# A third ready-made u tile in each attention head of a hybrid decoder layer

## The chip, the cores and the metric

The kernel runs on one core of one Trainium2 chip. The metric is the device time of one launch in microseconds (us), the median of several runs. TensorE (PE), VectorE (DVE), ScalarE (ACT), GpSimd (POOL) and SyncE (SP) run their own instruction streams and wait for each other on semaphores; SP, ACT and POOL issue DMAs.

## What is computed

One decoder layer on 512 tokens of width 2048: eight differential-attention heads and a short convolution side by side, an output projection, and then a PEER mixer that picks, per token and query head, 16 of 16384 single-neuron experts. The last step is this, cut from the reference:

```python
def one_block(args):
    hb, eb, gb = args
    ug = jnp.take(u, eb, axis=0)
    vg = jnp.take(v, eb, axis=0)
    act = jax.nn.gelu(jnp.einsum("tkd,td->tk", ug, hb), approximate=False) * gb.astype(hb.dtype)
    return jnp.einsum("tk,tkd->td", act, vg)
```

## The kernel before, in words

The program has five stages, one behind another: the projection to q, k and v; a loop over the eight heads, in which each head also computes one eighth of the convolution; the output projection; the *sweep*; and a dense stage with the v table.

**The sweep.** Instead of gathering u rows for three of the four token blocks, the kernel multiplies the whole u table with the hidden rows of 384 tokens: 128 tiles of 128 experts. A tile is loaded as rows (`u_tile`), but the product needs it turned (experts along the free side). TensorE turns a tile itself with 16 transposes of 128x128 (`turned`, L2054), in two halves of eight, between the two halves of the products of the tile before. `uT_hi` and `uT_lo`, the two parts that the product takes (three matmuls for one fp32 product, L1804 to L1806), are made by ACT and DVE from what was turned. The sweep is written as eight times 16 tiles; the eighth has neither new queries nor a choice of experts in it.

**Ready-made tiles.** Some tiles are turned long before the sweep, in the first three stages. SP loads the rows of a tile (`near_rows` or `far_rows`, one buffer each), DVE turns them with four STREAM_TRANSPOSE of 128x512 (`turn_rows`, L1295), and four DMAs of 256 KB store the result in `uT_all` in HBM (`store_turned`, L454), by SP or, in the heads, by POOL. `turned_before` says which tiles of the sweep these are: the odd ones below 2 * TURNED. TURNED is 56 before the change, so that the odd tiles 1 to 111 come ready-made, and in the eighth sweep of 16 TensorE turns every tile. For a ready-made tile `split_u` of ACT (L1112) and DVE (L1642) reads `u_tile` in SBUF; for the others it reads PSUM (L1117, L1647).

**A head.** Each head takes six conv pieces of 512 KB: SP loads piece p (`conv_piece`, L561) when piece p-2 has been split, ACT makes `wc_hi` (L910) and DVE `wc_lo` (`split_wc`, L1263). The order on DVE is written by hand: pieces 3 and 4 (counted from 0, so "the fifth piece" is number 4) at the head's start, then the softmax of four query blocks by `biased(qb)` (L1399 to L1404) and `combined(qb)` (L1411 to L1415), piece 5 and pieces 0 and 1 of the next head among them, then the norms of the head's output and of the next q and k, piece 2 of the next head, and the gating of the convolution. TensorE fills the waits of the attention with conv matmuls: conv(1, 1, 4, 10), for example, stands between the scores of blocks 0 and 1 and `turn_a(0)` (L1897), which waits for `combined(0)`.

Two tiles are made ready in a head. I call them by their place on DVE: before the change one is turned in two parts, behind `combined(0)` and behind `combined(1)`; the other behind the norm of the head's output, ahead of `norm_qk(j + 1, 1)`. Their rows come by `next_rows` (L468) behind the load that follows piece p = 2 and behind the one that follows p = 5; `next_rows` waits until the tile before it has been turned, since there is one row buffer. The turned rows have one buffer too: `turn_rows` waits for the store of the tile before. `keep_turned` on POOL stores them and stands in one stream with the inverse roots of the norms, the 16 DMAs that zero the gate grid and the stores of the mix. The last head makes no tile ready.

## Time and profile before

| | us |
|---|---|
| median of three runs | 2991.14 |
| lowest and highest | 2988.70, 2996.27 |
| the profiled execution: its time | 2991.42 |
| its span | 2989.6 |
| busy in the span: PE, DVE, POOL, ACT | 2897.0, 2357.7, 1495.1, 1049.9 |
| the heads' loop, from the q and k norm of head 1 to that of head 6 | 207.28 |

The span is the time from the first to the last instruction in the profile. A row of the timeline has start, duration, engine, line, operation, what is written and read, and in brackets how long the engine sat idle before it and what ended that. The chain of work is followed back from the last instruction to whatever released it, so it shows at each time what the end depended on.

### The profile page before, as it was taken

The page shows a single profiled execution, that of the slowest core. Times are in us where ns is not written, and L with a number is a line of the kernel's source. Part 1 is how long each engine was busy: PE and PEld are TensorE (multiplying, and loading weights), DVE is VectorE, ACT ScalarE, POOL GpSimd, SP SyncE. Part 2 cuts the span into 40 slices and gives each one's busy share as a digit, 9 for nine tenths or more (in the row PEclk, how much of TensorE's full clock was granted, in tenths as well). Part 3 has the DMA queues.
Part 4 walks back from the last instruction along what each step waited for, and adds up shares of the span by engine and source line. Part 5 has one row for each costly group of instructions (what it writes and reads, how often), then busy time and mean ns, then how long its engine had stood idle before and what let it go on. Part 6 is the DMA issues. An engine that isn't in the chain of part 4 may idle for free.

```text
span 2989.6 us, 40571 instructions
## 1 busy us (share of the span) xinstructions
PE 2897.0 (97%) x14993; PEld 2575.2 (86%) x14993; DVE 2357.7 (79%) x3038; ACT 1049.9 (35%) x1373; POOL 1495.1 (50%) x906
## 2 busy tenths in 40 slices
PE   8999999999999999999999999999999999899998
PEld 6887777778889999999999999999997877777787
DVE  6445677755678888888888898899768998898898
ACT  4111433341323333433333343334223433333333
POOL 1000232200015656565565656566868887778662
PEclk9999999999999999999999999999999999999999
DMA  8998777778758998989999899999999999999998
GB/s 301 331 351 273 229 237 241 223 300 311 243 180 298 315 340 291 339 302 327 319 305 340 290 333 316 317 349 353 339 353 409 413 414 414 414 415 416 416 410 355
DMA packets 333295, 980.65 MB, mean 328 GB/s; under 512 B 63764, under 2 KB 180512, under 8 KB 241760
## 3 DMA queue, kind: packets, MB, share of 16 engines
q1 hardware_dynamic: 188560, 508.60, 46.3%
q0 software_dynamic: 107008, 439.75, 41.2%
q10 hardware_dynamic: 37584, 30.43, 3.1%
q8 instruction: 86, 1.41, 0.2%
q14 instruction: 57, 0.47, 0.0%
HBM read 866.33 MB, written 112.33 MB: 327 GB/s over the span
## 4 chain that ended last, share of the span: by engine, by line
PE 66%; DVE 14%; DMA 11%; issue 4%; ACT 3%; SPq 1%; ACTq 0%; DVEq 0%; POOL 0%
PE ps L1804 21%; PE ps L1806 20%; PE ps L1805 20%; DMA v_raw<-in_peer_v 8%; PE ps L2054 3%; DVE x_rows L1662 2%; DMA wc_raw<-in_w_in 2%; DVE v_lo L1704 2%; DVE u_row L1653 2%; ACT v_hi L1173 1%; DVE uT_lo L1642 1%; DVE x_one L1754 1%; DVE near_turned L1295 1%; DVE uT_lo L1647 1%; PE ps L1904 1%
## 5 line engine op out<-in xcount | busy, mean ns | idle before, releaser
L1804 PE MATMUL ps<-hT_hi,uT_hi 128*128 128x384 f32 x2048 | 701.0, 342 | 21.2 <-DVE uT_lo L1642 19.0
L1806 PE MATMUL ps<-h2T_lo,uT_hi 128*128 128x384 f32 x2048 | 688.0, 336 | 0.0
L1805 PE MATMUL ps<-hT_hi,uT_lo 128*128 128x384 f32 x2048 | 687.0, 335 | 0.0
L815 POOL DMA_INDIRECT gate_grid<-gates,grid_cells x256 | 524.6, 2049 | 107.5 <-issue 78.8
L1804 PE MATMUL ps<-v_hi,a_hi 128*128 128x512 f32 x1024 | 403.7, 394 | 35.5 <-DVE v_lo L1704 34.9
L1804 PEld LDWEIGHTS ps<-hT_hi,uT_hi 128*128 128x128 f32 x2048 | 386.2, 189 | 30.9 <-DVE uT_lo L1642 24.8
L1173 ACT ACTIVATE v_hi<-v_raw 128x2048 fp32r<-128x2048 f32 x128 | 245.7, 1919 | 453.0 <-PE ps L1806 338.6
L1805 PE MATMUL ps<-v_hi,a_lo 128*128 128x512 f32 x1024 | 401.1, 392 | 0.0
L1806 PE MATMUL ps<-v_lo,a_hi 128*128 128x512 f32 x1024 | 401.0, 392 | 0.0
L1805 PEld LDWEIGHTS ps<-hT_hi,uT_lo 128*128 128x128 f32 x2048 | 386.6, 189 | 1.9
L1806 PEld LDWEIGHTS ps<-h2T_lo,uT_hi 128*128 128x128 f32 x2048 | 386.0, 188 | 0.0
L834 POOL DMA_INDIRECT v_ring<-in_peer_v,experts x128 | 291.3, 2276 | 135.8 <-DVE x_one L1754 103.8
L1704 DVE TENSOR_TENSOR v_lo<-v_raw,v_hi 128x2048 fp32r<-128x2048 f32 x128 | 293.2, 2291 | 72.9 <-ACT v_hi L1173 69.7
L805 POOL DMA_INDIRECT v_row<-in_peer_v,experts x128 | 147.6, 1153 | 341.3 <-DVE x_rows L1662 309.4
L1754 DVE SCALAR_TENSOR_TENSOR x_one<-v_ring,acts,x_one 128x2048 f32<-128x2048 f32 x128 | 300.5, 2347 | 3.2 <-DVE acts L1739 2.2
L1662 DVE SCALAR_TENSOR_TENSOR x_rows<-v_row,acts,x_rows 128x2048 f32<-128x2048 f32 x128 | 300.1, 2344 | 0.8 <-ACT acts L1126 0.8
L1653 DVE CUSTOM_DVE_ANT_0 u_row<-u_row,h_rows 128x2048 f32<-128x2048 f32 x128 | 292.5, 2285 | 0.0
L823 POOL DMA_INDIRECT dots<-products_one,cells x128 | 259.8, 2030 | 39.0 <-issue 39.0
L1804 PEld LDWEIGHTS ps<-v_hi,a_hi 128*128 128x128 f32 x1024 | 194.0, 189 | 83.8 <-issue 34.2
L1647 DVE TENSOR_TENSOR uT_lo<-ps,uT_hi 128x1024 fp32r<-128x1024 f32 x144 | 176.2, 1224 | 111.7 <-ACT uT_hi L1117 103.5
L1117 ACT ACTIVATE uT_hi<-ps 128x1024 fp32r<-128x1024 f32 x144 | 148.0, 1028 | 319.4 <-PE ps L2054 282.8
L1804 PE MATMUL ps<-w_hi,hT_hi 128*128 128x512 f32 x624 | 244.0, 391 | 0.8 <-DVE wi_lo L1249 0.8
(207 smaller groups left out, 4958.7 us busy)
## 6 DMA issues: line engine op xcount, KB each, us to landing
v_raw<-in_peer_v SPq DMA_DIRECT2D x128, 1024.0 KB
u_tile<-in_peer_u SPq DMA_DIRECT2D x72, 1024.0 KB
u_tile<-uT_all SPq DMA_DIRECT2D x56, 1024.0 KB
near_rows<-in_peer_u SPq DMA_DIRECT2D x40, 1024.0 KB, 8.3
uT_all<-near_turned SPq DMA_DIRECT2D x100, 256.0 KB, 7.0
w_raw<-in_w_in SPq DMA_DIRECT2D x24, 1024.0 KB, 9.2
wc_raw<-in_w_in SPq DMA_DIRECT2D x48, 512.0 KB, 7.4
far_rows<-in_peer_u SPq DMA_DIRECT2D x16, 1024.0 KB, 9.4
```

Source lines behind the costliest of these rows:

```text
L815: pool.indirect_dma_start(out=gate_grid, out_offset=bass.IndirectOffsetOnAxis(ap=grid_cells[:, d, col:col + 1], axis=0), in_=gates[:, 2 + ...
L823: pool.indirect_dma_start(out=dots[:, s:s + 1], out_offset=None, in_=products_one, in_offset=bass.IndirectOffsetOnAxis(ap=cells[:, col:col ...
L834: pool.indirect_dma_start(out=v_ring[s % RING][:, :], out_offset=None, in_=v_table, in_offset=slot(1, h, s)).then_inc(v_in[s % RING], 16)
L1173: nc.scalar.activation(v_hi[b % 2][:, :], v_raw[b % RAW_RING][:, :], ACT.Copy).then_inc(v_hi_ready, 1)
L1647: v.tensor_tensor(uT_lo[half][:, :, :], ps_uT[half], uT_hi[half][:, :, :].bitcast(F32), ALU.subtract)\
L1653: v.tensor_tensor_reduce(out=u_row[c % 2][:, :], in0=u_row[c % 2][:, :], in1=h_rows[:, 0, :], scale=1.0, scalar=0.0, op0=ALU.mult, op1=ALU ...
L1662: v.scalar_tensor_tensor(out=x_rows[:, 0, :], in0=v_row[c % 2][:, :], scalar=acts0[:, b:b + 1], in1=x_rows[:, 0, :], op0=ALU.mult, op1=ALU ...
L1704: v.tensor_tensor(v_lo[b % 2][:, :], v_raw[b % RAW_RING][:, :], v_hi[b % 2][:, :].bitcast(F32), ALU.subtract).then_inc(v_lo_ready, 1)
L1754: v.scalar_tensor_tensor(out=x_one[:, :], in0=v_ring[s % RING][:, :], scalar=acts[:, s:s + 1], in1=x_one[:, :], op0=ALU.mult, op1=ALU.add) ...
L1804: mm(out, a_hi, b_hi, start=first, stop=False)
L1805: mm(out, a_lo, b_hi, start=False, stop=False)
L1806: return mm(out, a_hi, b_lo, start=False, stop=last)
```

## The change

Three tiles a head are made ready instead of two, so TURNED goes from 56 to 63, and the odd tiles 113 to 125 of the eighth sweep come ready-made as well. Tile 127 does not. The new place is in front of `split_wc(j, 4)`, in one part; the tile that was turned in two parts is now turned in one, behind `combined(1)`; the place behind the norm stays.

```diff
-KEPT_BY_POOL = 1 + 2 * (HEADS - 1)
+KEPT_BY_POOL = 1 + 3 * (HEADS - 1)
@@ SP @@
-                    if p in (2, 5):
-                        next_rows(NEAR, 2 * j + (NEAR_HEADS + p // 5))
+                    if p in (2, 4, 5):
+                        next_rows(NEAR, 3 * j + (NEAR_HEADS + (2, 4, 5).index(p)))
@@ POOL @@
                 if j < HEADS - 1:
-                    keep_turned(NEAR_HEADS + 1 + 2 * j)
+                    keep_turned(NEAR_HEADS + 1 + 3 * j)
+                    keep_turned(NEAR_HEADS + 2 + 3 * j)
...
-                    keep_turned(NEAR_HEADS + 2 + 2 * j)
+                    keep_turned(NEAR_HEADS + 3 + 3 * j)
@@ DVE @@
+                if not last:
+                    turn_rows(NEAR, 3 * j + (NEAR_HEADS + 1), "heads")
                 split_wc(j, 4)
...
                 combined(0)
-                if not last:
-                    turn_rows(NEAR, 2 * j + (NEAR_HEADS + 1), "heads", range(2))
                 biased(2)
                 combined(1)
                 if not last:
-                    turn_rows(NEAR, 2 * j + (NEAR_HEADS + 1), "heads", range(2, 4))
+                    turn_rows(NEAR, 3 * j + (NEAR_HEADS + 2), "heads")
                 biased(3)
...
                 if not last:
-                    turn_rows(NEAR, 2 * j + (NEAR_HEADS + 2), "heads")
+                    turn_rows(NEAR, 3 * j + (NEAR_HEADS + 3), "heads")
```

DVE at the start of a head, before (`wc_lo<-wc_raw_129` is piece 4, `alibi` and `conv_taps` are two small steps ahead of it; ISA rows are waits and parts of instructions):

```order
L1263 TENSOR_TENSOR wc_lo<-wc_raw_130,wc_hi 128x1024
L1387 TENSOR_SCALAR alibi<-alibi 128x512
L1388 ISA
L1388 COPY conv_taps<-vec 128x3
L129 ISA
L1262 REGISTER_ALU
L1263 TENSOR_TENSOR wc_lo<-wc_raw_129,wc_hi 128x1024
```

And with the change:

```order
L1264 TENSOR_TENSOR wc_lo<-wc_raw_130,wc_hi 128x1024
L1388 TENSOR_SCALAR alibi<-alibi 128x512
L1389 ISA
L1389 COPY conv_taps<-vec 128x3
L129 ISA
L1287 ISA
L1291 ISA
L1296 STREAM_TRANSPOSE near_turned<-near_rows 128x4x4x32 x4
L1263 REGISTER_ALU
L1264 TENSOR_TENSOR wc_lo<-wc_raw_129,wc_hi 128x1024
```

Two waits (for the rows, L1287, and for the store of the tile before, L1291) and four transposes now stand ahead of piece 4, and so ahead of the whole softmax of the head.

SP in the loop over the heads, behind the load that follows p = 4, with the change (before, neither the two ISA rows nor the load of `near_rows` stand here):

```order
L561 DMA wc_raw_129<-in_w_in 128x8x128
L473 ISA
L468 ISA
L468 DMA near_rows<-in_peer_u 128x2048
L572 REGISTER_ALU
L561 ISA
L561 DMA wc_raw_130<-in_w_in 128x8x128
```

The load of the second tile's rows is put between piece 0 and piece 1 of the next head. The load for the first tile stays where it was, behind piece 4.

## Rows read from the trace of the kernel before

**Rows 1.** The page: span of the profiled execution.
```profile
span 2989.6 us, 40571 instructions
```

**Rows 2.** Chain of work over the whole span (start us, us, what).
```profile
336.68 1.23 DVE qk_ss L1379
...
543.96 1.23 DVE qk_ss L1379
```

**Rows 3.** Chain of work through head 3, 420 to 462 us.
```profile
426.56 7.56 DMA wc_raw<-in_w_in
...
434.23 1.07 ACT wc_hi L910
...
438.96 0.36 DVE probs L1415
...
439.37 0.33 PE ps L1897
```

**Rows 4.** Timeline of DVE, 415 to 462 us.
```profile
432.05 0.63 DVE L1388 COPY conv_taps<-vec 128x3 f32 x1
435.32 1.23 DVE L1263 TENSOR_TENSOR wc_lo<-wc_raw,wc_hi 128x1024 fp32r<-128x1024 f32 x1 [2.64 <-ACT wc_hi L910]
...
439.23 1.30 DVE L1295 STREAM_TRANSPOSE near_turned<-near_rows 128x512 f32<-128x512 f32 x2
...
446.72 0.69 DVE L1399 CUSTOM_DVE_ANT_0 probs<-ps,alibi 128x512 f32<-128x512 f32 x1 [2.16 <-PE ps L1897]
```

**Rows 5.** Instructions on near_rows, window 427 to 428 us.
```profile
L468 SPq DMA_DIRECT2D near_rows<-in_peer_u x1: 1962/1962/1962, 427.3 to 427.3; - x1
...
DMA to landing us min/median/max: 10.2/10.2/10.2
```

**Rows 6.** The same in head 1, window 343 to 346 us.
```profile
DMA to landing us min/median/max: 9.9/9.9/9.9
```

**Rows 7.** The same in head 3, window 448 to 455 us.
```profile
L468 SPq DMA_DIRECT2D near_rows<-in_peer_u x1: 346/346/346, 451.8 to 451.8; - x1
...
DMA to landing us min/median/max: 5.7/5.7/5.7
```

**Rows 8.** Timeline of PE before turn_a(0) of head 3.
```profile
438.50 0.39 PE L1806 MATMUL ps<-hT_lo,wc_hi 128*128 128x512 f32 x1
439.37 0.33 PE L1897 MATMUL ps<-ident,probs 128*128 128x128 f32 x1 [0.48 <-DVE probs L1415]
```

**Rows 9.** Timeline of DVE in head 0: its piece 4.
```profile
309.11 1.23 DVE L1263 TENSOR_TENSOR wc_lo<-wc_raw,wc_hi 128x1024 fp32r<-128x1024 f32 x1 [5.32 <-ACT wc_hi L910]
```

**Rows 10.** Timeline of PE in the dense stage, after a stall.
```profile
2478.72 0.79 PE L1804 MATMUL ps<-v_hi,a_hi 128*128 128x512 f32 x1 [5.32 <-DVE v_lo L1704]
2479.31 0.63 PE L1805 MATMUL ps<-v_hi,a_lo 128*128 128x512 f32 x1
2479.73 0.63 PE L1806 MATMUL ps<-v_lo,a_hi 128*128 128x512 f32 x1
```

**Rows 11.** Windows: that stretch, all engines; PEclk is the granted clock.
```profile
2476.13:2482.94 6.81, 4.22 (x10) 3.36 (x11) 6.65 (x4) 2.56 (x3) 5.90 (x4) 0.50 1.02 421
```

**Rows 12.** Chain of work, seventh sweep of 16: uT_lo, every fourth tile.
```profile
1951.11 1.24 DVE uT_lo L1642
...
2065.36 1.24 DVE uT_lo L1642
```

**Rows 13.** Timeline of PE, eighth sweep: the transposes of a tile's half.
```profile
2070.93 1.03 PE L2054 MATMUL ps<-ident,u_tile 128*128 128x128 f32 x8
...
2091.12 1.03 PE L2054 MATMUL ps<-ident,u_tile 128*128 128x128 f32 x8
```

**Rows 14.** Chain of work, 2030 to 2072 us: the same transposes.
```profile
2052.02 0.87 PE ps L2054 x8
```

**Rows 15.** Windows, seventh and eighth sweep: PE, PEld, DVE, ACT, POOL busy, PEclk, DMA.
```profile
1913.00:2065.00 152.00, 149.16 (x899) 146.43 (x898) 143.47 (x224) 60.77 (x98) 100.91 (x64) 1.00 0.98 346
2065.00:2235.00 170.00, 169.49 (x1068) 167.85 (x1067) 125.17 (x105) 54.25 (x90) 116.89 (x71) 1.00 0.97 350
```

## Prediction

> **What bounds the kernel now.** I read the page first, then the chain of work, then timelines of one head and of the last two sweeps. The profiled execution took 2991.42 us with a span of 2989.6 [rows 1]; the median of the three runs is 2991.14, 0.3 us below it, so I sum against 2991.4. TensorE is the busiest engine nearly everywhere, and the question is what the change does to the two places that it touches.
>
> *The heads.* Five heads, from the q/k norm of head 1 to that of head 6, take 207.3 us, or 41.5 us each [rows 2]. The chain through a head [rows 3] is to be read link by link: piece 4 is issued at 426.56 and takes 7.56 us; ACT splits it at 434.23, DVE makes its low part behind that (435.32, [rows 4]), does block 0 of the softmax until 439.32, and only then TensorE can turn block 0 at 439.37. TensorE was there earlier: its last conv matmul ahead of it began at 438.50, and it idled 0.48 us [rows 8]. So between 426 and 439 us DVE's order holds the head, with TensorE less than a us behind. DVE has one hole on this way, 2.64 us between `conv_taps` (ends 432.68) and piece 4 (starts 435.32), in which it waits for ACT [rows 4]. This hole is the room into which the change puts the new tile.
>
> *The sweep.* In the seventh sweep, where every second tile is ready-made, 12 tiles take 2065.36 - 1951.11 = 114.25 us, 9.52 a tile [rows 12]. In the eighth, where TensorE turns all, two tiles take 2091.12 - 2070.93 = 20.19 us, 10.10 a tile [rows 13], and TensorE is busy 169.49 of 170 us [rows 15].
>
> **The gain: seven tiles of the eighth sweep.** Seven tiles lose their 16 transposes. The lower price of a tile: a pair took 19.04 us with one ready-made and 20.19 with none, so 1.15 us. The upper: eight transposes hold the chain for 0.87 us [rows 14], 16 for 1.74. In the seventh sweep DVE was busy 143.47 of 152 us, because it also chose experts, and TensorE had to wait for it; in the eighth it is busy only 125.17 of 170 [rows 15], so it should keep up better. I take 1.4 a tile, 7 x 1.4 = 10 us, with 8 and 12 as ends. ACT and DVE split a ready-made tile with instructions of the same kind on SBUF, at no extra price, covered by DVE's 45 free us. The u loads of the sweep stay the same in number and size.
>
> **The cost: the new place in front of piece 4.** The transposes alone would be free. Two take 1.30 us, so four take 2.6 [rows 4], and the hole is 2.64. But they need the rows, and the rows have come too late for it. The load that feeds this place is the one behind p = 2, and it is in the kernel already: issued at 427.28 behind piece 4, it landed 10.2 us later [rows 5], at 437.5. Before the change nobody noticed, as the first transposes came at 439.23 [rows 4]. Now DVE waits at its new place until 437.5, turns until 440.1, and then starts on piece 4, for 435.32 before: 4.8 us later. All of block 0's softmax is queued behind it, and TensorE behind that, so I charge the whole 4.8. The load behind p = 2 has this landing in each of heads 1 to 6, from 9.9 us up [rows 6] and all within 0.4 us, since each has the same traffic around it: the store of the tile before, piece 4 ahead in SP's own queue, and the zeroing of the gate grid. None of that moves. Six heads make 6 x 4.8 = 28.8 us. Head 0 has a hole of 5.32 us ahead of piece 4, which ends at 309.11 for another reason [rows 9], and its load was issued at 293.7; I cost it at nothing. Head 7 turns nothing.
>
> **The second cost: TensorE's clock.** TensorE's wait ahead of block 0 grows from 0.48 to some 5.3 us. The trace has a stall of 5.32 us in the dense stage [rows 10]. Around it the granted clock is 0.50 for 6.8 us, the lower level of 1.2 GHz [rows 11], and the matmuls behind the stall start 0.42 us apart (2479.31 to 2479.73), where the conv matmuls of a head stand at some 0.23. Ten such matmuls were counted in that stretch [rows 11], so a stall costs 10 x 0.2 = 2.0 us more. TensorE is the bound behind `turn_a(0)`, so I charge it: 6 x 2.0 = 12 us, with 0 and 12 as ends. The Trainium skill ("TensorE: Matmul & The Clock Gate", Part 1) says that an idle TensorE is put back to 1.2 GHz; by that rule, the trace agrees.
>
> **The other edits.** *The two-part tile becomes one behind `combined(1)`.* DVE idled 2.16 us ahead of `biased(3)` [rows 4], which covers the extra 1.3 us of transposes there. But its rows are now loaded behind p = 4, some 2 us behind the new tile's transposes, so at about 442.5, and `combined(1)` is through at about 448 in the new times. The row nearest in a quiet stretch lands in 5.7 us [rows 7], at 448.2; one as slow as [rows 5] would land at 452.7, and with 2.6 us of transposes `biased(3)` would come about 4 us later than TensorE wants it. DVE also waits for the new tile's store, which POOL can issue only from 440.1 on. I take 0, because TensorE at the lower clock arrives 2 us later itself; the upper end is 3 us a head, 18 in all. *The third load* stands behind p = 5 as before. *POOL* issues four more DMAs a head; it waits in most of a head, and the inverse root queued behind them is due 10 us later. I cost them at nothing; if that cover went, the roots, the next q and k and piece 2 would be late. *Piece 0 of the next head* is issued 5 us later, as everything behind piece 4; it is not needed before the head's last third.
>
> **Sum.** 2991.4 - 10 + 28.8 + 12 = 3022.2 us.
>
> **Rivals.**
>
> *A. The stall without the clock.* The 5 us stalls fall so that the granted clock stays at full, as the clock is not lost in every idle moment. Then 2991.4 - 10 + 28.8 = 3010. Against it: the stall of the same length in [rows 10].
>
> *B. The rows come in time, and the change is faster.* Mechanism: the row load of p = 2 lands as fast as the one of p = 5, in 5.7 us [rows 7], so at 433.0. Then DVE turns from 433.0 to 435.6 and is 0.3 us late with piece 4. The point that decides is a landing by some 433 us: below it the transposes fit in the hole, above it every us is paid once a head. Time: 2991.4 - 10 + 6 x 0.3 = 2983. For it: longer heads leave DMA more air. Against it: the load still stands right behind piece 4, and in six of six heads it needed 10 us.
>
> *C. The second wait too.* The rows or the buffer of the middle tile are late as well: 3 us more a head, 3022 + 18 = 3040. For it: two more MB of traffic a head, in a stretch where the queues are full until 444 us.
>
> *D. POOL holds the eighth sweep.* POOL scatters all gates of that sweep in its first 11 tiles. If it cannot go faster than 10.1 us a tile, five of the seven tiles give nothing, and the gain is 3 instead of 10 us: 3029. Against it: busy 116.89 of 170 us [rows 15]. The Trainium skill ("GPSIMD Engine Reference", section 8) says that GpSimd shares its SBUF interfaces with VectorE and contends with DVE instructions that have two SBUF inputs, as DVE's dots and sums have; the rows can't say how much of POOL's busy time is such waiting.
>
> *E. The change does nothing.* The order says otherwise: TensorE's stream is shorter by the seven tiles' transposes. I give this no chance of its own.
>
> **How the numbers follow.** A measurement of this kernel tells some 0.3%, 9 us, from no change. The forecast as summed has 0.50, A 0.20, C 0.10, D 0.05: all are slower by more than 9 us, 0.85. B has 0.09, faster by 8 to 12 us, of which I count 0.01 as same. The remaining 0.06 is a mixture: the rows land 2 us sooner in the longer heads and the clock holds, 6 x 2.8 - 12 = +5, the same. So faster 0.08, same 0.07, slower 0.85. The range goes from 3002 (3.6 us a head, no clock, gain 10) to 3038 (nearly all of C).
>
> **What would show it.** Right: in heads 1 to 6 DVE idles about 5 us behind `conv_taps` with the near_rows DMA as what ended it; TensorE's turn of block 0 has 5 us of idle before it; a head takes 46 to 49 us; PEclk drops in the heads; the eighth sweep is about 10 us shorter. Wrong: a landing of the p = 2 rows below 7 us; a head at 42 us; or an eighth sweep that has not moved, which would point to POOL or DMA.

## The result and the profile after

| | before | with the change |
|---|---|---|
| median of the runs, us | 2989.92 (4 runs, 2988.42 to 2996.27) | 3056.05 (4 runs, 3049.62 to 3059.38) |
| ratio, with its 95% interval | | 1.0216 [1.0202, 1.0229] |
| span of the profiled execution, us | 2989.6 | 3053.4 |

The change costs 66 us, or 2.2%. The direction was forecast; the size was not, as 3056 lies 18 us above the upper end of the range. The two spans differ by 63.8 us, and the rows below say where they lie. Lines of the changed kernel are mostly one higher than before (the wait of `turn_a` is L1898 for L1897).

**The heads: +55.3 us.** The squares for the q/k norm are summed once a head, so the first and the last of these sums frame seven heads.

The kernel before, instructions on qk_ss (line, engine, operation and count, shortest/median/longest ns, first to last start):
```profile
L1379 DVE TENSOR_REDUCE qk_ss<-sq x8: 1220/1220/1222, 294.1 to 585.4; 128x16 f32<-128x1024 f32 x8
```
The changed kernel, the same view:
```profile
L1380 DVE TENSOR_REDUCE qk_ss<-sq x8: 1220/1221/1222, 294.2 to 640.8; 128x16 f32<-128x1024 f32 x8
```
Seven heads took 291.3 us and take 346.6. Head 0 has hardly a part in that: the six heads behind it went from 248.7 us (336.7 to 585.4) to 302.9 (337.9 to 640.8). That is 54.2 us, or 9.0 a head, for the 6.8 of the forecast.

The changed kernel, waits of PE, 338 to 641 us (who <- what ended it: us in total, times, longest):
```profile
PE ps L1898 <- DVE probs L1418: 33.5, 10, 6.7
PE ps L1905 <- ACT aT L967: 6.9, 6, 1.3
```
The kernel before, waits of PE, 337 to 586 us:
```profile
PE ps L1897 <- DVE probs L1415: 1.9, 5, 0.5
```
TensorE waited 1.9 us in these six heads and waits 40.4 now: 30.8 at the turn of block 0 (6.70, 4.98, 4.82, 4.34, 4.99 and 4.96 us in heads 1 to 6), 2.7 at later turns and 6.9 for `aT`, ACT's copy of the turned blocks. So 38.5 of the 54.2 us are idle time of TensorE. The rest, 15.7 or 2.6 a head, is time in which it works more slowly, as the windows over the six heads show (PE, PEld, DVE, ACT, POOL busy, then PEclk, DMA share, GB/s), first before, then with the change:
```profile
336.70:585.40 248.70, 246.65 (x1214) 194.99 (x1213) 182.56 (x397) 98.02 (x193) 70.00 (x85) 1.00 0.76 241
337.90:640.80 302.90, 262.51 (x1214) 202.37 (x1213) 196.90 (x420) 96.46 (x193) 83.07 (x109) 0.94 0.75 239
```
The same 1214 matmuls are busy for 262.5 us instead of 246.7, at a granted clock of 0.94 in the mean instead of 1.00.

The changed kernel, waits of DVE, 338 to 641 us:
```profile
DVE near_turned L1296 <- DMA near_rows<-in_peer_u: 48.6, 12, 6.4
```
Before, DVE never waited for rows in these heads. Now it waits twelve times, so twice a head.

The changed kernel, timeline of DVE in head 3 (start, duration, what, in brackets the idle before it and what ended it; its first row is the same `conv_taps` step as the first row of [rows 4], which now comes 20.6 us later):
```profile
452.69 0.63 DVE L1389 COPY conv_taps<-vec 128x3 f32 x1
457.84 2.49 DVE L1296 STREAM_TRANSPOSE near_turned<-near_rows 128x512 f32<-128x512 f32 x4 [4.52 <-DMA near_rows<-in_peer_u]
460.25 1.18 DVE L1264 TENSOR_TENSOR wc_lo<-wc_raw,wc_hi 128x1024 fp32r<-128x1024 f32 x1
...
472.67 2.49 DVE L1296 STREAM_TRANSPOSE near_turned<-near_rows 128x512 f32<-128x512 f32 x4 [3.38 <-DMA near_rows<-in_peer_u]
475.08 0.65 DVE L1402 CUSTOM_DVE_ANT_0 probs<-ps,alibi 128x512 f32<-128x512 f32 x1
```
Between `conv_taps` and piece 4's `wc_lo` there now lie 4.52 us of waiting and 2.49 of turning, for the 2.64 us hole of [rows 4]. That is the forecast's mechanism. The second wait, 3.38 us in front of the middle tile, is the one that the forecast had taken as 0; `biased(3)` (475.08) stands behind it.

The changed kernel, instructions on near_rows, 447 to 449 us, the answer to [rows 5]:
```profile
L468 SPq DMA_DIRECT2D near_rows<-in_peer_u x1: 1885/1885/1885, 447.9 to 447.9; - x1
...
DMA to landing us min/median/max: 9.8/9.8/9.8
```
The same at 462 to 463 us, the middle tile's load:
```profile
L468 SPq DMA_DIRECT2D near_rows<-in_peer_u x1: 972/972/972, 462.3 to 462.3; - x1
...
DMA to landing us min/median/max: 10.2/10.2/10.2
```
The first load takes the 10 us that were read from the kernel before; the second, for which [rows 7] had suggested 5.7, takes 10.2.

The changed kernel, timeline of PE at the turn of block 0 in head 3:
```profile
464.37 0.47 PE L1898 MATMUL ps<-ident,probs 128*128 128x128 f32 x1 [4.82 <-DVE probs L1418]
```
And the window around it (PE, PEld, DVE, ACT, POOL busy, then PEclk, DMA share, GB/s):
```profile
459.00:465.80 6.80, 1.98 (x8) 0.81 (x6) 4.88 (x18) 2.25 (x9) 2.20 (x4) 0.72 1.05 354
```
The idle of 0.48 us in [rows 8] is 4.82, and the granted clock has a mean of 0.72 around it, so it is at 1.2 GHz for over half of those 6.8 us. The same window shows the DMA engines full (share 1.05).

**The eighth sweep: 5.3 us longer instead of 10 shorter.** ACT copies the product of each tile out of PSUM, so sixteen of these copies frame fifteen tiles. Instructions on products in the kernel before:
```profile
L1147 ACT ACTIVATE products<-ps x16: 490/492/492, 2086.3 to 2237.3; 128x384 f32<-128x384 f32 x16
```
The same in the changed kernel:
```profile
L1148 ACT ACTIVATE products<-ps x16: 490/492/493, 2144.0 to 2300.3; 128x384 f32<-128x384 f32 x16
```
They took 151.0 us and take 156.3.

The changed kernel, waits of DVE in this stretch:
```profile
DVE u_row L1654 <- DMA u_row<-in_peer_u,experts: 25.9, 9, 5.5
DVE x_rows L1663 <- DMA v_row<-in_peer_v,experts: 9.4, 4, 3.6
```
DVE never waited for a gathered row there before; now it waits 35.3 us for `u_row` and `v_row`. POOL issues these gathers, between its scatters of the gates.

The changed kernel, windows: the stretch in three parts (PE, PEld, DVE, ACT, POOL busy, PEclk, DMA share, GB/s):
```profile
2144.00:2210.00 66.00, 65.63 (x399) 64.73 (x399) 50.94 (x37) 23.27 (x37) 53.95 (x28) 1.00 0.97 341
2210.00:2262.00 52.00, 46.42 (x256) 44.70 (x255) 31.99 (x24) 14.44 (x25) 44.99 (x24) 0.93 0.93 308
2262.00:2300.30 38.30, 33.19 (x198) 31.91 (x196) 25.05 (x20) 8.68 (x16) 18.99 (x13) 1.00 0.94 348
```
In the first part TensorE has hardly a gap: its seven tiles took 65.5 us, for 70.7 before. In the second it stands still for 5.6 us of 52, and this is POOL's part: 24 issues are busy for 44.99 us, and with the 0.30 us that lies between two of them (7.2 in all) they fill the 52 us to the last. The next five tiles took 56.3 us, for 50.5. In the third part there are hardly any scatters left (the last is issued at 2269.94), but the gathered rows are still late: the last three tiles took 34.5 us, for 29.9. In the chain of work two gathers of `v_row` stand there with 9.15 and 13.68 us from issue to landing. So 4.7 of the 5.3 us come when the scatters are all but over; why the loop doesn't catch up there, no run shows.

The changed kernel, groups of POOL's instructions over the whole stretch (busy us, mean ns, idle before and what ended it):
```profile
L816 POOL DMA_INDIRECT gate_grid<-gates,grid_cells x32 | 73.6, 2299 | 9.7 <-issue 9.7
L801 POOL DMA_INDIRECT u_row<-in_peer_u,experts x15 | 26.3, 1755 | 14.7 <-DVE dots L1654 11.0 <-issue 3.7
L806 POOL DMA_INDIRECT v_row<-in_peer_v,experts x16 | 19.3, 1207 | 14.2 <-issue 8.9 <-DVE x_rows L1663 5.3
```
The same in the kernel before:
```profile
L815 POOL DMA_INDIRECT gate_grid<-gates,grid_cells x32 | 58.6, 1832 | 9.7 <-issue 9.7
L805 POOL DMA_INDIRECT v_row<-in_peer_v,experts x15 | 30.9, 2062 | 26.5 <-DVE x_rows L1662 18.0 <-issue 8.5
L800 POOL DMA_INDIRECT u_row<-in_peer_u,experts x15 | 14.8, 987 | 13.6 <-DVE dots L1653 9.9 <-issue 3.7
```
The same 32 scatters cost POOL 15 us more than before, while the gathers' issues together stay at 45.6 us (45.7 before).

The remaining 3 us of the 63.8 lie in the stretches between: 1.8 from the heads to the first product of the sweep, 0.5 in the first seven sweeps, 0.8 in the dense stage, each no more than one execution differs from another.

### The profile page after: what moved, and what is told of

It reads as the page before. It is cut to its first block, busy times and chain, and to the rows that moved or that the text cites. A ratio compares the mean times of both kernels' runs of the same rounds, so it can differ in the third digit from the quotient of the medians.

```text
span 3053.4 us, 40459 instructions
## 1 busy us (share of the span) xinstructions
PE 2911.7 (95%) x14881; PEld 2580.2 (85%) x14881; DVE 2375.2 (78%) x3066; ACT 1049.7 (34%) x1373; POOL 1522.3 (50%) x934
## 4 chain that ended last, share of the span: by engine, by line
PE 57%; DVE 16%; DMA 12%; issue 6%; POOL 5%; ACT 3%; SPq 0%; ACTq 0%; DVEq 0%; POOLq 0%
PE ps L1805 18%; PE ps L1807 18%; PE ps L1806 18%; DMA v_raw<-in_peer_v 6%; DVE x_rows L1663 3%; DMA near_rows<-in_peer_u 3%; PE ps L2055 2%; DVE u_row L1654 2%; POOL gate_grid L816 2%; DMA wc_raw<-in_w_in 2%; DVE v_lo L1705 2%; DVE near_turned L1296 1%; DVE uT_lo L1643 1%; ACT v_hi L1174 1%; POOL dots L824 1%
## 5 line engine op out<-in xcount | busy, mean ns | idle before, releaser
L816 POOL DMA_INDIRECT gate_grid<-gates,grid_cells x256 | 535.3, 2091 | 107.4 <-issue 78.8
L806 POOL DMA_INDIRECT v_row<-in_peer_v,experts x128 | 135.1, 1055 | 331.8 <-DVE x_rows L1663 306.0
L824 POOL DMA_INDIRECT dots<-products_one,cells x128 | 267.2, 2088 | 49.1 <-issue 38.7
L801 POOL DMA_INDIRECT u_row<-in_peer_u,experts x128 | 176.4, 1378 | 151.0 <-DVE dots L1654 75.5
L454 POOL DMA_DIRECT2D uT_all<-near_turned x88 | 48.5, 558 | 404.1 <-DVE near_turned L1296 403.0
```

Source lines behind the costliest of these rows:

```text
L801: pool.indirect_dma_start(out=u_row[b % 2][:, :], out_offset=None, in_=u_table, in_offset=slot(0, i, b)).then_inc(u_in[b % 2], 16)
L816: pool.indirect_dma_start(out=gate_grid, out_offset=bass.IndirectOffsetOnAxis(ap=grid_cells[:, d, col:col + 1], axis=0), in_=gates[:, 2 + ...
L824: pool.indirect_dma_start(out=dots[:, s:s + 1], out_offset=None, in_=products_one, in_offset=bass.IndirectOffsetOnAxis(ap=cells[:, col:col ...
```

## The experiments

Sixteen kernels, on chips where the kernel before took between 2991.65 and 2993.66 us in the median. Five take the sweep apart, the others the heads; *heads* below is the time from the first to the last sum of squares (291.3 us before, 346.6 with the change), and *eighth sweep* that of fifteen tiles (151.0 and 156.3). Both are read from the one profiled execution of each kernel; that of s1 was the slowest of its ten (3002.80 us) and that of s3 the slowest of its six, so their sweeps are long by some us.

| run | median, us | ratio [95%] | heads | eighth sweep |
|---|---|---|---|---|
| s1_sweep_only | 2995.50 | 1.0018 [1.0007, 1.0028] | | 159.8 |
| s2_low_from_psum | 2995.71 | 1.0018 [1.0007, 1.0030] | | 152.5 |
| s3_scatter13 | 3001.95 | 1.0038 [1.0025, 1.0050] | | 161.5 |
| s4_half_scatters | 2978.81 | 0.9956 [0.9939, 0.9972] | | 140.1 |
| c1_before_half_scatters | 2992.45 | 1.0000 [0.9988, 1.0013] | | 150.6 |
| h1_heads_only | 3051.13 | 1.0201 [1.0181, 1.0221] | 348.6 | 150.6 |
| h2_first_rows_small | 3054.58 | 1.0211 [1.0193, 1.0230] | 347.3 | |
| h3_second_rows_small | 3029.35 | 1.0120 [1.0103, 1.0137] | 331.3 | |
| h4_both_rows_small | 3030.55 | 1.0134 [1.0118, 1.0151] | 325.2 | |
| h5_zeroing_in_last_head | 3084.64 | 1.0312 [1.0295, 1.0330] | 350.8 | |
| h6_small_rows_ahead | 3022.34 | 1.0093 [1.0072, 1.0113] | 321.0 | |
| h7_full_rows_ahead | 3069.18 | 1.0256 [1.0233, 1.0280] | 364.2 | |
| h8_no_rows | 3018.49 | 1.0088 [1.0071, 1.0105] | 318.7 | |
| h9_small_rows_no_zeroing | 3022.85 | 1.0099 [1.0082, 1.0116] | 290.6 | |
| g1_other_places | 3022.65 | 1.0103 [1.0086, 1.0120] | 316.5 | 154.3 |
| g4_places_zeroing_last | 3058.79 | 1.0215 [1.0197, 1.0234] | 319.7 | 154.3 |

### The two parts of the change apart

**s1_sweep_only.** The kernel before, in which the sweep takes tiles 113 to 125 as ready-made. Their rows are those of tile 111, read again.
```diff
-    return tile % 2 == 1 and tile < 2 * TURNED
+    return tile % 2 == 1 and tile < 2 * (TURNED + 7)
...
-                    source = uT_all[tile // 2 * P:(tile // 2 + 1) * P, :] if turned_before(tile)\
+                    source = uT_all[min(tile // 2, TURNED - 1) * P:(min(tile // 2, TURNED - 1) + 1) * P, :] if turned_before(tile)\
```


> The kernel before, with only the sweep changed: the odd tiles 113 to 125 are also taken as ready-made (they re-read the stored rows of tile 111, so the products of these seven tiles are not the reference's); no third tile is made in the heads. Theory 1 (the missing 10 us were lost in the eighth sweep itself, where GpSimd cannot issue faster): the eighth sweep of 16 takes about 156 us instead of 151, GpSimd is busy nearly all of its first 11 tiles, and the time is 2 to 8 us above before. Rival (the sweep gains 8 to 12 us as I forecast, and the changed kernel lost it by something that the heads left behind): the eighth sweep takes about 141 us and the time is 8 to 12 us below before.

2995.50 us, 1.0018 [1.0007, 1.0028] of before. The gain isn't there even with heads that are as before: it is lost in the sweep itself, and nothing that the heads do takes it away.

**h1_heads_only.** The changed kernel, all 63 tiles made and stored, but the sweep uses the first 56.
```diff
-    return tile % 2 == 1 and tile < 2 * TURNED
+    return tile % 2 == 1 and tile < 2 * (TURNED - 7)
```


> The changed kernel with all its new work in the heads, but the sweep takes only the 56 tiles of before as ready-made, so that the seven new ones are made and not used. Theory 1 (the heads cost 55 us by themselves, and nothing in the sweep pays it back): heads 1 to 6 take 50 us each, the eighth sweep 151 us as before, and the time is 53 to 58 us above before. Rival (part of the loss needs the changed sweep, or the extra stores of the heads slow later stages): more than 3 us of the difference to before lies behind the heads.

3051.13 us: the heads alone cost some 60 us. So the two parts, 59 and 4 us over before, come to 63 of the change's 66. All heads runs below start from this kernel, if nothing else is said.

### The sweep: who holds it

**s2_low_from_psum.** As s1, but DVE makes `uT_lo` of the seven tiles from PSUM, as for the tiles that TensorE turns.
```diff
-                if turned_before(c):
+                if turned_before(c) and c < 2 * TURNED:
```


> As s1_sweep_only, but for the seven new ready-made tiles VectorE takes the low part from the PSUM bank (whatever stands there) instead of from u_tile in SBUF, so that its subtraction has one SBUF input and not two; the low part of these tiles is then not the reference's. Same instructions, same order. Theory A (GpSimd is held off by VectorE instructions with two SBUF inputs, of which the ready-made tiles add two a tile): GpSimd's gate_grid instructions get shorter than in s1_sweep_only, the eighth sweep falls from 156 to 148 us or less. Rival B (GpSimd is slow because the tiles come faster and its 3 scatters and 2 gathers a tile meet full DMA queues): the eighth sweep takes the same as in s1_sweep_only within 2 us.

2995.71 us, to s1's 2995.50. The two single profiles differ (152.5 and 159.8 us), the medians of the runs don't. So the source of the low part makes no difference in time that these runs can tell, and this edit does not bring the gain back.

**s3_scatter13.** As s1, with the last 32 scatters over 13 tiles instead of 11.
```diff
-                    tiles = TOPK - 1 if i < PEER_HEADS - 1 else 11
+                    tiles = TOPK - 1 if i < PEER_HEADS - 1 else 13
```


> As s1_sweep_only, but the last sweep's 32 scatters are spread over 13 tiles instead of 11, so 2.46 instead of 2.91 a tile. Theory 1 (GpSimd's issue time a tile sets the eighth sweep): it falls by some 0.45 x 2.3 us a tile in the first 11 tiles, so by about 10 us to 146 us, and the time is below before by some 5 us, unless the last scatters then come too late for the first weights of the dense stage. Rival (the bound in the eighth sweep is DMA bandwidth, not issue): no change to s1_sweep_only, as the bytes are the same.

3001.95 us, slower than s1 by 6. The expectation missed. With thinner scatters nine early tiles run at some 9.2 us instead of seven, but the last scatter is over only at 2227 us and the first dense gates are loaded behind it, at 2229. DVE waits 15.0 us for them in the last tile, which takes 24.7 us. The work of POOL was moved, not made less.

**s4_half_scatters.** As s1, with every second scatter of the eighth sweep left out.
```diff
+                        if i == PEER_HEADS - 1 and n % DENSE == 1:
+                            continue
```


> As s1_sweep_only, but the eighth sweep issues 16 of its 32 scatters of gates (those of one of the two dense token blocks are left out, so its gates are wrong); each moves 128 values of 4 bytes, so the bytes hardly change. Theory 1 (GpSimd's issuing time bounds the eighth sweep with ready-made tiles): VectorE no longer waits for u_row, the 16 tiles take 138 to 143 us, and the time is 8 to 13 us below before, which is the gain I forecast. Rival (DMA queues or HBM bound it): still 150 us or more.

2978.81 us, 0.9956 [0.9939, 0.9972]: now the seven tiles pay.

s4_half_scatters, instructions on products in the eighth sweep:
```profile
L1149 ACT ACTIVATE products<-ps x16: 491/492/497, 2083.5 to 2223.6; 128x384 f32<-128x384 f32 x16
```
And the window over them:
```profile
2083.50:2223.60 140.10, 139.66 (x848) 138.23 (x848) 107.58 (x80) 46.01 (x77) 80.86 (x47) 1.00 1.02 380
```
TensorE is busy 139.66 of 140.1 us, and the DMA engines move 380 GB/s, for 333 in s1's sweep, with nearly the same bytes (53.25 and 53.35 MB). So neither TensorE, nor DVE, nor the bytes to be moved were what held s1. The edit takes two things away together, sixteen issues of POOL and their 4-byte packets (of packets under 512 B there are 3614 instead of 5930), and no run parts them. That it is the issues rests on the window 2210 to 2262 of the changed kernel above, which POOL's issues fill to the last.

**c1_before_half_scatters.** The control: the kernel before with the same half of the scatters left out.

> The kernel before with only 16 of the 32 gate scatters in the eighth sweep (half of that sweep's gates are left out). Control for the run with both the ready-made tiles and half the scatters, which was 12 us faster than before. Theory 1, before the change the eighth sweep is TensorE's: 151 us as before, time within 0.1% of before (2989 to 2993). Rival, GpSimd's issues already cost the kernel before some us, so that the halving alone is the gain: eighth sweep 145 us or less, time 2984 or less.

2992.45 us, 1.0000 [0.9988, 1.0013], eighth sweep 150.6 us. This half of the scatters costs the kernel before nothing. Halved scatters alone gain nothing, seven tiles alone gain nothing, and both together gain 13 us. The eighth sweep of the kernel before is held by TensorE at 10.1 us a tile and, not far below that, by POOL's issues: in its first eleven tiles POOL waits for others only 10.7 of 109.7 us, which leaves 9.0 us of its own a tile. From c1 to s4 fifteen tiles lose 150.6 - 140.1 = 10.5 us, so a ready-made tile is worth 1.5 us to TensorE.

### The heads: which transfer is late, and behind what

**h2_first_rows_small.** The first tile's load is cut to 64 bytes a partition and issued ahead of piece 4.
```diff
+                    if p == 2:
+                        few_rows(NEAR, 3 * j + NEAR_HEADS)
                     conv_piece(j + (p + 2) // PIECES, (p + 2) % PIECES)
-                    if p in (2, 4, 5):
+                    if p in (4, 5):
```
`few_rows` is `next_rows` with columns 0 to 15.

> As h1_heads_only, but the load for the tile in front of piece 4 brings only 64 bytes a partition and is issued ahead of piece 4, so that the rows are there when VectorE comes (the tile is turned from old rows and not used). All transposes and stores stay. Theory 1 (the rows' late landing is what costs in front of piece 4, and the transposes fit in the hole): TensorE's wait before turn_a(0) falls from 4.9 to under 1 us, the lower clock goes with it, heads 1 to 6 take 42 to 44 us, and the time is 3 to 15 us above before. Rival (the 2.6 us of transposes ahead of the softmax cost by themselves): 2 to 3 us of that wait stay in each head, with a part of the low clock, and a head takes 45 us or more.

3054.58 us, and the heads are as long as before this edit: 347.3 us for 348.6. The expectation missed by all of it.

h2_first_rows_small, DVE in head 3, in front of the first and of the middle tile:
```profile
451.36 2.49 DVE L1303 STREAM_TRANSPOSE near_turned<-near_rows 128x512 f32<-128x512 f32 x4 [0.26 <-DVE conv_taps L1396]
...
470.31 2.49 DVE L1303 STREAM_TRANSPOSE near_turned<-near_rows 128x512 f32<-128x512 f32 x4 [8.38 <-DMA near_rows<-in_peer_u]
```
The first wait is gone, and the second has grown from 3.9 us (head 3 of h1) to 8.4. DVE is early at the middle tile now, but its rows are not: the load took 14.3 us. The first wait was only the first of two stops in front of the same backlog.

**h3_second_rows_small.** The middle tile's load is cut instead, in its place behind piece 0 of the next head.

> As h1_heads_only, but the load for the tile behind combined(1) brings only 64 bytes a partition; the load in front of piece 4 is whole. Theory 1 (the second tile's rows come late too, and this is the part of the heads' cost that I did not charge): TensorE's waits of 0.7 to 2 us before turn_a(2) or turn_a(3) and before apply_v(3) go, the 4.9 us before turn_a(0) stays, and heads 1 to 6 take 48.0 to 49.0 us instead of 50.7. Rival (those waits come from the store of the first tile or from the lower clock, not from the rows): a head still takes 50 us or more.

3029.35 us, heads 47.7 to 48.9 us each, as expected for one wait taken away: in head 3 DVE waits 4.9 us at the first tile and 0.2 at the middle one.

**h4_both_rows_small.** Both cut, each in its place behind a piece.

> The changed kernel's heads with the sweep of before; the row loads of the first and of the middle tile of each head (behind p = 2 and behind p = 4) carry 64 bytes a partition instead of 8 KB, so that both land at once and two of the three 1 MB row loads of a head are gone (the tiles are then turned from mostly old rows). Theory 1, the heads' loss is the two late landings and the clock that goes with them, and the turns themselves are all but free: heads of 41.5 to 43 us, no idle of TensorE over 1.5 us ahead of the turn of block 0 or of block 2, time 2990 to 3000. Rival, the extra transposes on DVE (7.5 us a head instead of 5) or POOL's extra issues cost by themselves: heads of 44 us and more with the rows there in time, time over 3005.

3030.55 us, heads of 47 us: in the median no better than h3, where 42 was expected. Two of three megabytes a head are gone, and DVE still waits 33.2 us for rows.

h4_both_rows_small, instructions on wc_raw, 448 to 449 us: the piece behind p = 4 in head 3, which is piece 0 of the next head.
```profile
L566 SPq DMA_DIRECT2D wc_raw<-in_w_in x1: 373/373/373, 448.3 to 448.3; - x1
...
DMA to landing us min/median/max: 10.5/10.5/10.5
```
Instructions on near_rows, 448.5 to 450 us: the 8 KB behind it.
```profile
L473 SPq DMA_DIRECT2D near_rows<-in_peer_u x1: 1551/1551/1551, 449.0 to 449.0; - x1
...
DMA to landing us min/median/max: 10.0/10.0/10.0
```
448.3 + 10.5 = 458.8 and 449.0 + 10.0 = 459.0: 8 KB land 0.2 us behind the 512 KB that stand ahead in SP's queue. In this place 8 KB take as long as the full 1 MB (10.2 us in the changed kernel). The Trainium skill ("DMA: Bandwidth & Descriptors", SWDGE vs HWDGE vs iDMA) says that inside a DMA engine the transfers issued by GpSimd and those of SP and ACT stand in different queues, between which it goes round. By that, a load waits for what SP issued before it and shares with what POOL issued. The trace is in line with it: here the 8 KB wait for the piece, and in h9 below they land 5.0 us behind the piece that was ahead of them, with a 1 MB store of POOL issued 1.1 us before them.

**h5_zeroing_in_last_head.** The gate grid is zeroed in heads 0 and 7 only.
```diff
-                for n in range(2 * j, 2 * j + 2):
+                for n in range(*{0: (0, 2), HEADS - 1: (2, ZERO_DMAS)}.get(j, (0, 0))):
                     zero_cells(n)
```


> The changed kernel's heads with the sweep of before; the gate grid's 16 zeroing DMAs of 1 MB are issued in head 0 (2) and in the last head (14) instead of two in each head. Theory 1, the row loads are late because they share the DMA engines with this head-start backlog: in heads 1 to 6 the rows of the first tile land 6 to 7 us after their issue instead of 10, the wait ahead of the turn of block 0 falls from 5 us to under 1.5, heads of 43 to 46 us, and the last head and the output projection get longer by what 14 MB cost there. Rival, the row load is slow by itself because it stands behind the 512 KB piece in SP's queue and the store of the tile before: landing stays at 9 to 10 us and the heads at 49 to 51.

3084.64 us. The heads stay at 51, and the first tile's rows still land 9.9 us after their issue (499.4 us in that trace, with no zeroing near it), so for them the rival was right: their 10 us don't come from the zeroing, which is issued later. What stands ahead of them is the store of the tile before and piece 4; no run takes these away from a full load, so their part is argued. The middle tile's 1 MB don't land sooner either.

h5_zeroing_in_last_head, instructions on near_rows, 514 to 516 us: the middle tile's load in head 4.
```profile
DMA to landing us min/median/max: 10.3/10.3/10.3
```
In the changed kernel it was 10.2, there with the zeroing issued 10.7 us ahead of it. The time is 33 us over h1, and 29 of them are there by the first product of the sweep: behind the heads under comparison stand the 14 MB of zeroing now.

**h6_small_rows_ahead.** Both loads small, and both issued ahead of their pieces.

> The changed kernel's heads with the sweep of before; the row loads of the first and of the middle tile carry 64 bytes a partition, and both are issued ahead of the conv piece that they followed (the tiles are then turned from mostly old rows). With the same small loads behind the pieces, they landed within 0.2 us of the 512 KB piece in front of them in SP's queue. Theory 1, what holds the heads is only when rows land, and a load cannot land ahead of what was issued before it: now both are there when DVE wants them, no wait of DVE for rows over 1 us, no idle of TensorE over 1.5 us at the turns of blocks 0 and 2, heads of 42 to 43.5 us, time 2992 to 3002. Rival, the turns on DVE or POOL's issues hold the heads as well: no wait for rows, but heads of 45 us and more, time over 3010.

3022.34 us, heads of 45.7 to 47.7. The first wait is gone, the middle one is not.

h6_small_rows_ahead, waits of DVE, 336 to 615 us:
```profile
DVE near_turned L1305 <- DMA near_rows<-in_peer_u: 25.4, 6, 4.6
```
The middle tile's 8 KB, issued at 444.5 us in head 3:
```profile
DMA to landing us min/median/max: 11.1/11.1/11.1
```
Piece 5, ahead of them in SP's queue, was issued at 439.7 and took 15.8 us in this run, with the zeroing in flight, so the 8 KB landed 0.1 us behind it.

**h7_full_rows_ahead.** The order of h6 with the full 1 MB.

> The same order, with the row loads at their full 1 MB: all rows as in the changed kernel, only each issued ahead of its piece instead of behind it. Theory 1, the sum of what is queued decides: rows of the first tile land some 2 to 3 us sooner, piece 4 lands 3 us later, and DVE waits for the one or the other; heads of 48 to 51 us, time 3030 to 3050. Rival, the order alone was the fault: heads of 45 us or less, time under 3015.

3069.18 us, heads of 52.7 to 54.1, worse than expected. In head 4 the rows landed 6.9 us after their issue, in time, but piece 4, now behind them, took 16.5 us, and TensorE waits 61.4 us in six heads. A better order inside SP's queue only picks which transfer is late.

**h8_no_rows.** Neither row load is issued; SP raises their semaphore. Turns and stores stay.
```diff
+                    if p == 2:
+                        no_rows(NEAR, 3 * j + NEAR_HEADS)
+                    if p == 4:
+                        no_rows(NEAR, 3 * j + (NEAR_HEADS + 1))
```


> The changed kernel's heads with the sweep of before; the row loads of the first and of the middle tile are left out altogether (SP raises their semaphore instead, ahead of the piece), so that both tiles are turned and stored from old rows in their places, with no wait for a DMA of rows. All twelve stores, all twelve turns and POOL's issues stay. Theory 1, the landing of rows is the whole loss: no idle of DVE for rows, TensorE's idle at the turns of blocks 0 and 2 under 1.2 us, no low clock, heads of 41.5 to 43.5 us, time 2990 to 3003. Rival, the 2.5 us more of turns or the store behind them cost a head 2 us and more by themselves: heads of 44 us and more, time over 3007.

3018.49 us, heads of 45.5 to 46.9. Theory 1 as I had put it, that the rows' landing is the whole loss, falls here.

h8_no_rows, waits of DVE, 336 to 613 us:
```profile
DVE near_turned L1304 <- DMA uT_all<-near_turned: 23.8, 7, 4.7
```
With no wait for rows, DVE waits just as long at the middle tile for the *store* of the first, since there is one buffer for turned rows. That store is issued 5 us behind 2 MB of zeroing.

**h9_small_rows_no_zeroing.** h6 with h5's edit.

> The run with both row loads cut to 8 KB and issued ahead of their pieces, with the gate grid's zeroing moved from heads 1 to 6 to the last head. In that run the middle tile's 8 KB, issued at 444.55 us, landed 11.1 us later, behind 2 MB of zeroing issued at 438.6 and 439.4. Theory 1, it is this backlog that holds the middle tile's rows: they land in 5 to 7 us, DVE's wait of 4.5 us for them falls under 1, heads 1 to 6 of 42 to 44 us (the last head and the stage behind it are longer, as in the other run with the zeroing moved). Rival, the store of the first tile and piece 5, which are issued just ahead, hold it alone: landing still 9 us and more, heads of 45.5 us and more.

h9_small_rows_no_zeroing, instructions on qk_ss:
```profile
L1389 DVE TENSOR_REDUCE qk_ss<-sq x8: 1220/1220/1222, 294.0 to 584.6; 128x16 f32<-128x1024 f32 x8
```
Its waits of DVE, 336 to 585 us, all that it has on near_turned:
```profile
DVE near_turned L1305 <- DVE conv_taps L1398: 1.6, 6, 0.3
DVE near_turned L1305 <- DMA uT_all<-near_turned: 0.8, 2, 0.7
```
And the window over six heads:
```profile
335.70:584.60 248.90, 247.11 (x1213) 194.66 (x1212) 194.89 (x420) 97.30 (x193) 72.56 (x97) 1.00 0.68 190
```
Heads of 41.5 us, as in the kernel before, with three tiles turned and stored in each: TensorE busy 247.11 of 248.9 us, granted clock 1.00. This settles the heads. The third turn on DVE, the four more stores and POOL's four more issues cost nothing here; all that the heads lost is transfers that land late, and the clock that goes with them. The middle tile's 8 KB landed in 5.4 us, for 11.1 in h6, and piece 5 in 4.8, for 15.8. The whole kernel still took 3022.85 us, since the zeroing came back behind the heads: from 584.6 to the first product of the sweep it is 324.7 us, for 295.0 before. No cut was free here. The zeroing matters for these small loads; for the full ones h5 shows that taking it away alone is worth nothing. What h9 takes away is the zeroing and 2 MB of rows a head together. It is not the mean load of the DMA engines in the heads that tells this: their share is 0.76 before and 0.75 with the change.

### A better place?

**g1_other_places.** All 63 tiles with full rows, turned behind `combined(1)`, behind `combined(3)` and behind the gating of the convolution, their loads behind p = 3, p = 4 and p = 0 of the next head.
```diff
-                    turn_rows(NEAR, 3 * j + (NEAR_HEADS + 1), "heads")
                 split_wc(j, 4)
...
                 combined(1)
+                    turn_rows(NEAR, 3 * j + (NEAR_HEADS + 1), "heads")
...
                 combined(3)
+                    turn_rows(NEAR, 3 * j + (NEAR_HEADS + 2), "heads")
...
                 v.tensor_tensor(b_sb, conv_y, b_sb, ALU.mult).then_inc(conv_out, 1)
+                    turn_rows(NEAR, 3 * j + (NEAR_HEADS + 3), "heads")
```


> The whole change (63 ready-made tiles, all used, right result), with the three tiles at other places: behind combined(1), behind combined(3), and behind the gating of the convolution at a head's end; each row load is issued behind the piece after which the buffer is free, so no turn is ahead of the softmax or of the next q and k norm. Theory 1 (the heads' cost is one of place, not of the third tile's work or traffic): no wait over 1 us before turn_a(0), heads 1 to 6 at 41 to 43 us; the eighth sweep as in s1_sweep_only; time within 10 us of before, 50 us under the changed kernel. Rival (a head has no room for a third tile, its transposes or its 2 MB more of traffic come back as a wait elsewhere): heads at 44 us or more.

3022.65 us, 33 us better than the change and 31 worse than before. The heads take some 45 us, and TensorE waits 19.3 us in six of them (1.9 before), most of it in `apply_v` for a block whose softmax stands behind a turn. The eighth sweep took 154.3 us: as in the change, nothing gained.

**g4_places_zeroing_last.** g1 with the zeroing in the last head.

> All 63 tiles, turned at the other places of a head (behind block 1, behind block 3, behind the gating of the convolution, with their loads behind p = 3, p = 4 and p = 0 of the next head), and the zeroing of the gate grid moved to the last head as well. Theory 1: what was left in the heads of that version (45 us against 41.5) was waits for rows and stores behind the zeroing, so heads 1 to 6 come to 42 to 43.5 us; with the last head some us longer and no gain in the eighth sweep the time is 3000 to 3015. Rival: the heads stay at 45, since three 1 MB row loads and twelve stores are themselves more than a head has room for; time 3025 to 3035.

3058.79 us, and heads 1 to 6 stay at 45.2 to 46.7. The heads are the rival's; the time is 24 us above even its forecast, which had no price in it for 14 MB of zeroing behind the heads. With full rows no version here found room in a head, with or without the zeroing, and none beats the kernel before. A second buffer for the rows or for the turned rows, which would let loads be issued earlier, was not tried.

## Why the prediction was wrong

**The time** was 3022 and is 3056. Against the working's own sum, in its order:

- *The gain, 7 x 1.4 = 10 us: the step that failed most.* The price of a tile was right: 1.5 us, from c1 to s4. But it was taken as a gain in time, while it is one of TensorE's work. Against rival D stood "busy 116.89 of 170 us", and this misled in two ways. It is a mean over 16 tiles, of which the last five have no scatters; and the 0.30 us ahead of each issue are not in it. In the first eleven tiles of the kernel before POOL was busy 85.82 of 109.70 us, and 50 issues with 0.30 us each make that about 101. D's own case, no gain in the eleven tiles, had a chance of 0.05 and was still too mild: the sweep got 5.3 us longer, most of it in the last three tiles. Error: 15 us.
- *The new place, 4.8 us x 6.* Right in mechanism and in size. DVE's wait was 4.52 us in head 3, the landing 9.8 us, near the 10.2 of [rows 5], and TensorE's idle at the turn of block 0 came to 30.8 us in six heads, for at most 1.9: some 4.8 more a head.
- *The other edits, 0: failed.* "I take 0, because TensorE at the lower clock arrives 2 us later itself" was the step. The middle tile's rows landed in 10.2 us, not in the 5.7 of [rows 7], a row from the quiet end of a head. The second wait was 3.38 us for DVE. TensorE's idle grew by 38.5 / 6 = 6.4 us a head; with 4.8 for the first wait, 1.6 are left for what stands behind the second, so 10 us in six heads. This is rival C, which had 3 us a head and a chance of 0.10.
- *The clock, 2.0 us x 6 = 12.* The clock fell as forecast, and [rows 10] and [rows 11] were a fair model of one stall. The six heads lost 15.7 us, most likely because each had a second stall that was not counted; no run shows this by itself.
- *Head 0 at nothing, head 7, the third load, POOL's issues, the sweep's u loads at nothing.* All right: head 0 grew by 1.1 us, and h9 shows turns, stores and issues to be free.

The sum forecast 31 us more, the spans differ by 63.8. Of the 33 us that are missing, 13 lie in the six heads (4.8 + 1.6 + 2.6 = 9.0 us each for 6.8), 1 in head 0, 15 in the sweep, and 3 in the stretches between.

**The reason for the 10 us** was in part wrong. The store, piece 4 ahead and the zeroing were named, and h5 shows that the zeroing has no part in the first load's landing, nor in the middle one's as long as the rows are full (10.3 us without it, 10.2 with it). It comes in only where the loads are small and DVE gets to the middle tile sooner (11.1 us in h6, 5.4 in h9).

**The range** took the two failed steps one at a time: its upper end was C without D. In both a price was read in another stretch than the one it was for: POOL's from a mean over sixteen tiles, the landing from the quiet end of a head. C and D together, priced by the text's own numbers, give 3047; with the sweep slower than before, 3056.

## What to carry over

Before an engine's free share is spent, look at the stretch in which the new load must fit, and at the queue of each engine that has a fixed amount of work per step there: taking work from the busiest engine gains only up to the next one, and c1 and s4, half the neighbour's work with and without the change, show the limit in two runs. A load's landing can depend more on its place in the queues than on its size (8 KB and 1 MB both took 10 us in one place); read it from a transfer in the same place, and count on a second wait to grow by what the first one gives back. And removing one wait at a time says little when several stand in front of one backlog: h2, h4, h6 and h8 each took something away and found the next, h5 alone changed nothing, and only h9 took away all of it.

## What the runs showed of the hardware

**POOL's issues stretch while DVE computes.** The changed kernel, timelines of POOL and of DVE in the eighth sweep:
```profile
2250.47 2.56 POOL L801 DMA_INDIRECT u_row<-in_peer_u,experts  x1 [0.30 <-issue]
2253.33 0.96 POOL L806 DMA_INDIRECT v_row<-in_peer_v,experts  x1 [0.30 <-issue]
2254.60 1.61 POOL L816 DMA_INDIRECT gate_grid<-gates,grid_cells  x1 [0.30 <-issue]
2256.52 1.58 POOL L816 DMA_INDIRECT gate_grid<-gates,grid_cells  x1 [0.30 <-issue]
2258.40 3.13 POOL L816 DMA_INDIRECT gate_grid<-gates,grid_cells  x1 [0.30 <-issue]
```
```profile
2249.80 2.35 DVE L1663 SCALAR_TENSOR_TENSOR x_rows<-v_row,acts,x_rows 128x2048 f32<-128x2048 f32 x1
2253.09 1.22 DVE L1648 TENSOR_TENSOR uT_lo<-ps,uT_hi 128x1024 fp32r<-128x1024 f32 x1 [0.95 <-ACT uT_hi L1118]
2257.80 2.29 DVE L1654 CUSTOM_DVE_ANT_0 u_row<-u_row,h_rows 128x2048 f32<-128x2048 f32 x1 [3.48 <-DMA u_row<-in_peer_u,experts]
```
A gather's issue takes 0.96 us beside a subtraction that reads PSUM (2253.09) and 2.56 beside a sum over `x_rows`. A scatter's takes 1.61 with DVE quiet, 1.58 where the dot begins only while it runs, and 3.13 where the dot is running already. The issue at 2250.47 ends 0.88 us behind the sum's end at 2252.15, as if it had begun only there. This is regular: in the eighth sweep of both kernels 48 issues begin while DVE is inside a dot or a sum, and 47 of them end a fixed time behind that instruction's end, the 19 gathers 0.81 to 0.88 us and 28 of the 29 scatters 1.42 to 1.48. The Trainium skill ("SBUF — State Buffer", SBUF: two separate sides) says that a GpSimd operation that reads SBUF and a DVE instruction with two SBUF inputs lock each other out of a shared port for a whole instruction; by that rule, the trace agrees. This also makes the loop feed on itself: POOL's rows come late, DVE runs its dots and sums at other times, and the same 32 scatters took 73.6 us instead of 58.6. That the stretching turned a missing gain into 5.3 us of loss is argued from these rows; no run took it away by itself.

**A small load is not a quick one.** 8 KB took 10.0 us (h4) and 11.1 us (h6), both behind a 512 KB piece and with 2 MB of zeroing issued 5 to 8 us before them, and 5.4 us without the zeroing (h9).

**Stalls of 3 us took the clock too.** h6_small_rows_ahead, window around TensorE's idle of 3.02 us in head 3:
```profile
458.00:466.00 8.00, 4.99 (x16) 3.93 (x15) 6.69 (x16) 3.45 (x7) 2.19 (x4) 0.65 0.66 161
```
The granted clock averages 0.65 over these 8 us, so TensorE ran at 1.2 GHz for most of them. The forecast had only a row with 5.32 us of idle to go by.
